# The gate's blocks in the scan of the large mixer: whole behind every fourth value, or in halves behind every other

## What is computed

```
proj = hn @ w_in
z, xbc, dt_raw = split(proj)                 # z: 2048 features, the gate
xbc = silu(conv5(xbc)); xs, bm, cm = split(xbc)
dt = softplus(dt_raw + dt_bias); log_a = -exp(a_log) * dt
y = scan forward + scan backward of (cm, bm, xs * dt, log_a)   # 32 heads of 64
y = (y + xs * d_skip) * silu(z)
y = y * rsqrt(mean(y * y over each of 4 groups) + eps) * norm_g
out = y @ w_out
```

## Time and profile before

| | us |
|---|---|
| median of 3 runs | 2640.28 (2639.51 to 2641.73) |
| the profiled execution, device time | 2640.01 |
| its span, first to last instruction | 2638.2 |
| TensorE busy in the span | 2606.0 |
| the scan, value 0 to the end of value 63 | 831.3 to 1001.1 |

### The profile page before, as it was taken

How to read it: one execution, slowest core, us unless ns; L and a number is a source line. 1 busy time by engine, 2 the same in 40 slices (tenths; PEclk the granted TensorE clock), 3 DMA queues, 4 the chain that set the end, 5 groups by cost and what they waited for, 6 DMA issues and landing times.

```text
span 2638.2 us, 32995 instructions
## 1 busy us (share of the span) xinstructions
PE 2606.0 (99%) x11700; PEld 2023.6 (77%) x11700; DVE 1525.3 (58%) x2124; ACT 1178.6 (45%) x1858; POOL 252.2 (10%) x200
## 2 busy tenths in 40 slices
PE   9999999999999999999999999999999999999999
PEld 7854788888786557788888776788888777888887
DVE  4467677643988785677643787543333536533333
ACT  3326443433546894444333688532333425422332
POOL 0021100000103781100000230000000001000000
PEclk9999999999999999999999999999999999999999
DMA  5310333333244442233333220233333321333333
GB/s 211 96 56 2 107 98 96 95 96 95 82 136 123 125 128 80 80 97 97 99 97 96 94 64 1 79 98 99 97 95 95 104 80 49 95 96 96 98 99 97
DMA packets 71287, 246.03 MB, mean 93 GB/s; under 512 B 7420, under 2 KB 7548, under 8 KB 70816
## 3 DMA queue, kind: packets, MB, share of 16 engines
q1 hardware_dynamic: 70256, 236.43, 29.4%
q0 software_dynamic: 944, 8.46, 0.9%
HBM read 242.63 MB, written 2.24 MB: 93 GB/s over the span
## 4 chain that ended last, share of the span: by engine, by line
PE 90%; ACT 3%; DVE 3%; issue 2%; POOL 1%; DMA 1%; SPq 0%; DVEq 0%; ACTq 0%; POOLq 0%
PE bank L333 26%; PE bank L335 26%; PE bank L334 26%; PE bank L1698 1%; PE bank L881 1%; POOL xT L727 1%; PE bank L912 1%; PE bank L901 1%; PE bank L2521 1%; PE bank L535 1%; DVE over_hn L701 1%; PE bank L520 1%; PE bank L1705 1%; PE bank L521 0%; PE bank L1139 0%
## 5 line engine op out<-in xcount | busy, mean ns | idle before, releaser
L323 DVE TENSOR_TENSOR wlo<-wraw,whi 128x1024 fp32r<-128x1024 f32 x409 | 509.3, 1246 | 578.7 <-ACT whi L300 577.9
L333 PE MATMUL bank<-hnhi,whi 128*128 128x512 f32 x1952 | 779.1, 399 | 2.0 <-DVE arena L1548 1.2
L334 PE MATMUL bank<-hnlo,whi 128*128 128x512 f32 x1952 | 760.6, 390 | 0.0
L335 PE MATMUL bank<-hnhi,wlo 128*128 128x512 f32 x1952 | 760.4, 390 | 0.0
L300 ACT ACTIVATE whi<-wraw 128x1024 fp32r<-128x1024 f32 x409 | 430.3, 1054 | 536.9 <-DMA wraw<-in_w 536.7
L333 PE MATMUL bank<-ahi,whi 128*128 128x512 f32 x1184 | 463.0, 391 | 1.0 <-DVE alo L556 0.2
L335 PE MATMUL bank<-ahi,wlo 128*128 128x512 f32 x1184 | 460.7, 389 | 0.0
L334 PE MATMUL bank<-alo,whi 128*128 128x512 f32 x1184 | 460.7, 389 | 0.0
L333 PEld LDWEIGHTS bank<-hnhi,whi 128*128 128x128 f32 x1952 | 366.4, 188 | 109.7 <-issue 34.3
L334 PEld LDWEIGHTS bank<-hnlo,whi 128*128 128x128 f32 x1952 | 366.6, 188 | 80.5 <-issue 6.5
L335 PEld LDWEIGHTS bank<-hnhi,wlo 128*128 128x128 f32 x1952 | 366.4, 188 | 77.9
(11 more groups left out here) (299 smaller groups left out, 2502.2 us busy)
## 6 DMA issues: line engine op xcount, KB each, us to landing
wraw<-in_w SPq DMA_DIRECT2D x410, 512.0 KB, 3.6
arena<-cs_scratch SPq DMA_DIRECT2D x20, 512.0 KB, 6.3
over_a<-cs_scratch SPq DMA_DIRECT2D x12, 512.0 KB, 6.3
arena<-in_rpb POOLq DMA_DIRECT2D x1, 2880.0 KB, 14.4
out_dram<-xT SPq DMA_DIRECT2D x8, 256.0 KB, 2.0
arena<-in_t_step POOLq DMA_DIRECT2D x2, 897.0 KB, 4.7
arena<-in_t_ab POOLq DMA_DIRECT2D x1, 1536.0 KB, 6.9
xT<-in_x SPq DMA_DIRECT2D x2, 512.0 KB, 7.0
```

Of the source, the lines that this page charges most:

```text
L323: dve.tensor_tensor(wlo[:, slot * BLOCK:(slot + 1) * BLOCK], wraw[:, slot * BLOCK:(slot + 1) * BLOCK], whi[:, slot * BLOCK:(slot + 1) * BL ...
L333: pe.matmul(out, wh, ah, start=start, stop=False)
L334: pe.matmul(out, wh, al, start=False, stop=False)
L335: return pe.matmul(out, wl, ah, start=False, stop=stop)
```

## The change

`Z_STEPS` now lists 14 values, those behind which a block's second half stood, and `z_rows` issues all eight rows of a block there, 24 matmuls. `dve_z` keeps its places in VectorE's queue; only the way they are found from the list is rewritten.

```diff
--- before.py
+++ after.py
@@ -1454,7 +1454,7 @@
 
         Z0 = FIRST["c_in"] + 25
 
-        Z_STEPS = [q for q in range(60) if q % 2 == 0 and q not in (28, 44)]
+        Z_STEPS = [2, 6, 10, 14, 18, 22, 26, 32, 36, 40, 46, 50, 54, 58]
 
         def conv_tile(m):
             return tile(m + (31 if m.r is None and m.base < 9 else 7))
@@ -1724,8 +1724,7 @@
             for q in range(2 * SSD_HEADS):
                 value(q)
                 if q in Z_STEPS:
-                    i = Z_STEPS.index(q)
-                    z_rows(2 + i // 2, i % 2 * 4, i % 2 * 4 + 4)
+                    z_rows(2 + Z_STEPS.index(q), 0, KT)
                 if q % 16 >= 12 and q < 60:
                     scores(q // 16 + 1, q % 16 - 12)
                     pe_turn(pe, q // 16 + 1, q % 16 - 12)
@@ -1831,8 +1830,8 @@
                     dve_diagonal(dve, q // 4 * 2 + q % 4 + 1)
                 if q == 0:
                     dve_z(dve, 1)
-                if q - 2 in Z_STEPS and Z_STEPS.index(q - 2) % 2 == 1:
-                    dve_z(dve, 2 + Z_STEPS.index(q - 2) // 2)
+                if q - 2 in Z_STEPS:
+                    dve_z(dve, 2 + Z_STEPS.index(q - 2))
                 if q in (36, 38):
                     dve_gained(dve, At(q // 2 - 18))
             dve_low_part(dve, "c_out", At(0))
```

## The result

| | before | after |
|---|---|---|
| median, us | 2640.32 | 2664.14 (2663.78 to 2664.46, 4 runs) |
| profiled execution, us | 2640.01 | 2663.78 |
| its span, us | 2638.2 | 2662.0 |
| value 0 to value 63 (starts), us | 168.77 | 192.27 |
| mean granted clock | 1.000 | 0.997 |

The ratio is 1.0089, with a 95% interval of 1.0077 to 1.0101: the change makes the kernel 23.8 us slower. The forecast was +18.2 us, 2658.2, with a range of 2649 to 2666. The scan alone accounts for 23.5 us; what lies ahead of value 0 and behind value 63 is the same within 0.3 us. The forecast's time is met within 6 us, but not by its sum alone: 6.3 us of the loss come from a second cause that the forecast had put aside.

A forecast was written before the change was run, and what follows sets the result against it. The prediction took four engines as nearly full, TensorE fullest, with TensorE and VectorE waiting for each other once a quad. Its pieces from value to value summed to +18.2 us on 2640.0, 2658.2 us; range 2649 to 2666.

The forecast's parts named there:

- The loop of `dve_z`: T starts the first value behind a block; fourth value waits until T + 4.70, so a quad takes 11.45 us, 1.74 more.
- To value 3: Scan's start: value 2's probabilities, held by `dve_z` of block 1, then a value with a whole block: +1.7 us.
- Quads to 7 and 11: Quads (four values and one block) ending in the blocks at 6 and 10: 1.74 us each, +3.5.
- 14 to 18: Values 14 to 18: value 18's probabilities come from the new group's copies; +2.1 us, the same at 46 to 50.
- 18 to 26: Two quads, values 18 to 26, with a 4.85 us chain whose diagonal took 1.37: +2.9 us.
- 26 to 32: Values 26 to 32: no half block left in it, a 1.3 us wait of a turn should go; with the switch -1.5 us.
- 32 to 40: Values 32 to 40: `dve_z` stands behind two more steps, chains of 4.70 and 5.15 us; +2.2 us.
- 40 to 46: Values 40 to 46: ScalarE's decay of value 45 needs value 41; value 46 starts at T + 11.5; +2.3 us.
- 50 to 58: Two quads, values 50 to 58, taken as the same as values 18 to 26: +2.9 us.
- Rival 4: Granted clock falls to its lower level for the blocks, whose 78 us would double: 2718 us and more; chance 0.02.
- Rivals 1 to 3: Only the switches count, 2636.4 us, chance 0.05; faster, 2633.1, chance 0.04; half the loss, 2646.5, chance 0.09.
- Rival 2: Faster, if VectorE has the fourth value's probabilities by T + 2.7 against 4.70: -6.9 us, 2633.1; chance 0.04.

The follow-up runs named there:

- Experiment 3: Kernel after with `dve_z` one value later and the skip term moved behind the diagonal of the fourth value; 2649.68 us, ratio 1.0034 to the kernel before.
- experiment 1: Kernel after with `dve_z` alone moved one value later in VectorE's queue; 2659.67 us, ratio 1.0075 to the kernel before.
- experiment 4: Kernel after with three filler matmuls on constants before the fourth value behind a block, where `q % 16 < 12`; 2659.6 us, ratio 1.0074 to the kernel before.
- experiment 6: experiment 4 with five more filler matmuls ahead of the turn behind value 45; 2661.77 us, ratio 1.0077 to the kernel before.
- experiment 5: Kernel before with only the blocks finished behind values 2, 6, 10 and 14 whole; 2644.79 us, ratio 1.0015 to the kernel before.
- experiment 2: Kernel after with only the skip term moved, to behind the diagonal of the fourth value; 2653.14 us, ratio 1.0051 to the kernel before.
- experiment 8: Half blocks behind 2, 18, 46 and 50, whole ones elsewhere, with `dve_z` and skip term late in whole quads; 2648.8 us, ratio 1.0037 to the kernel before.
- experiment 9: Kernel before with only the block behind value 32 whole; 2638.11 us, ratio 0.9990 to the kernel before.
- experiment 7: Experiment 3 with filler matmuls ahead of values 18, 36, 40, 50 and the turn behind value 45; 2647.93 us, ratio 1.0028 to the kernel before.

## Why the prediction was right, and where not

- **What bounds the scan**: right. The loop of `dve_z`, four steps of VectorE, one value and a whole block closed as described; the order of waits in the trace after is the one named. Experiment 3 shows it by its absence. That it has two ties, `dve_z` and the skip term, was not said. It makes no difference to the sum, since both lie on the same chain, but it would have misled whoever moved `dve_z` alone (experiment 1). The scan was to take about 188 us; it took 193.3, and 187.0 without the four falls.
- **To value 3**: 1.7 forecast, 1.62 measured. **Quads to 7 and 11**: 1.74 each forecast, 1.37 and 1.39 measured. The term that was mis-sized is the diagonal in the chain: 1.06 us was taken from the earlier trace rows, and 0.75 is what it took. The Trainium skill, SBUF — State Buffer, Who interferes with whom, says that a VectorE instruction with two SBUF inputs contends with a GpSimd instruction that reads SBUF, and the traces agree: where a GpSimd instruction is well under way as the diagonal begins, the diagonal ends 0.60 to 0.64 us behind that one's end (14 times before, 5 after), and else it lasts 0.73 to 0.76. In the quads to 7, 11, 23 and 27 it now came ahead of GpSimd's instruction and took 0.75; in those to 55 and 59 it did not, and took 1.67 and 1.69. So the rule's hint to the lower half held for four quads of six. **Quad to 15**: 0 forecast, -0.10 measured.
- **14 to 18**: +2.1 forecast and 3.70 measured, of which 1.6 is the clock; experiment 4, with no fall there, has 2.06. The same for **46 to 50**: 2.1, 3.68, and 2.08 in experiment 4.
- **18 to 26**: +2.9 forecast, 1.56 measured. Here the price of the diagonal (1.37) was wrong the same way: the two quads took 11.08 and 11.10 us where 11.75 was reckoned. **26 to 32**: -1.5 forecast, -1.54 measured.
- **32 to 40**: +2.2 forecast, 2.93 measured. The two chains took 4.85 and 5.78 us, not 4.70 and 5.15, mostly by the split of weights in the second. Its row before, and after:

```profile
939.55 1.21 DVE L323 TENSOR_TENSOR wlo<-wraw,whi 128x1024 fp32r<-128x1024 f32 x1
...
947.09 1.94 DVE L323 TENSOR_TENSOR wlo<-wraw,whi 128x1024 fp32r<-128x1024 f32 x1
```

- **40 to 46**: +2.3 forecast (its own terms add up to T + 11.4, not 11.5, so to +2.2); 3.89 measured with a fall of the clock, 2.34 in experiment 6 without one.
- **50 to 58**: +2.9 forecast, 5.01 measured, of which 1.6 are the clock; the rest is two quads of 12.0 us (the fall left aside) where 11.75 was reckoned, as the diagonal took its long form. In the quad to 55 it began beside a GpSimd instruction:

```profile
995.37 1.28 POOL L1635 TENSOR_TENSOR arena<-arena,mT 128x512 f32<-128x512 f32 x1 [1.37 <-ACT mT L1739]
...
995.58 1.67 DVE L1541 COPY_PREDICATED mT<-arena,mT 128x512 f32<-128x512 uint32 x1
```

- **The clock**: wrong. Rival 4 had 0.02, as the stretch 215 to 245 kept its clock with TensorE busy 26.3 of 30 us, and it was priced as all or nothing. The Trainium skill, TensorE: Matmul & The Clock Gate, A second HAM failure mode, tells of a kernel whose TensorE idles briefly and often between groups of matmuls and so moves between its two clocks; the trace after agrees, with waits of 1.9 to 2.3 us ahead of all four falls, though two more waits of 1.9 us brought none. What came was four short falls of 1.6 us. Without them the loss is 23.5 - 6.3 = 17.2 us, against 18.2 forecast. So two errors partly cancel: the chain was sized too long by 1 us in sum, and the clock was left out. Within the sum there is luck too: four quads were reckoned 2.0 us too long, and 32 to 40 and 50 to 58 came out 1.2 us too short.
- **The range** held the time, 2 us from its upper end, for a reason that it did not allow for: the clock. Its own terms, all taken one way, give 11.0 to 26.1 us and not 12 to 25. **Rivals 1 to 3**: experiment 5 rules out that the loss of the first four blocks is given back, and experiment 3 gives the saving by the switch in a covered quad as 0.46 us, more than the 0.26 that was reckoned. Rival 2's condition, the fourth value's probabilities ready by T + 2.7, is met in experiment 3, and the quads were indeed faster than before. The kernel was not, for the changes of group.

What stays open: why a wait brings a fall in one kernel and not in another. In experiment 2 value 18 waited 1.9 us as in the kernel after, and the clock stood; in experiment 8 it stood through two waits of 2.9 us in the profiled execution, while the others had a lower mean clock. The fillers show that fewer waits leave fewer falls, not which wait brings one.

## What to carry to other kernels

When filler work is spread between steps that other engines prepare, its grain sets how far ahead those engines have to be: doubling the grain here wanted the fourth value 2.8 us earlier. Look for every instruction in the preparing engine's queue that waits for what the filler, or the first step behind it, completes; each of them turns the preparation into a chain behind the block. Put the large grain where the preparing engine is late anyway and gets its input sooner for it (one case here, experiment 9), and leave the small grain where it has no lead.

## What the runs showed of the hardware

- TensorE's granted clock fell to its lower level in stretches of 3.4 us in a kernel whose longest wait of TensorE was some 2.3 us and whose scan had TensorE busy for 171.5 of 193.3 us. In the kernel before, with 166.1 of 169.8, it did not. A long wait alone does not bring a fall: two of 1.9 us in the same trace and two of 2.9 us in that of experiment 8 brought none. Each fall lengthened its piece by 1.5 to 1.6 us, as a matmul starts every 0.43 instead of 0.23 us; where the next value waits for VectorE anyway, part of that is hidden (experiment 7).
- Filler matmuls on constants inside the waits made the kernel 4.5 us faster; in the trace three falls less give 4.8 us and the fillers take back some 1.3 (experiment 4).
- The same diagonal (128x512, predicated copy) lasted 0.75, 1.06, 1.37, 1.57 and 1.67 us in the rows shown, with the same shape of operands. Its length follows the GpSimd instruction that is under way as it begins: it ends 0.60 to 0.64 us behind that one's end (19 times in the traces before and after; 996.65 and 997.25 in the rows of the quad to 55). Where none is, or none with more than 0.15 us left, it lasts 0.73 to 0.76 us.
